# Gathering U and V rows apart: two rings in place of one in a mixture-of-single-neurons layer

## The reference

```python
q = (xt @ w_query).reshape(t, PEER_HEADS, 2, PEER_HALF)          # 8 heads
sk = jnp.einsum('thcd,ckd->thck', q, sub_keys)                    # 2 x 128 keys
top_s, top_i = lax.top_k(sk, PEER_TOPK)                           # 16 of each
cand_s, cand_i = all 16 x 16 sums and their expert numbers
best_s, best_pos = lax.top_k(cand_s, PEER_TOPK)                   # 16 experts per token and head
gate = jax.nn.softmax(best_s, axis=-1)
h = jnp.einsum('thkd,td->thk', peer_u[ib], xb)                    # a dot with a gathered U row
a = gb * jax.nn.gelu(h)
out = jnp.einsum('thk,thkd->td', a, peer_v[ib])                   # a sum of gathered V rows
```

## Time and profile before

| | us |
|---|---|
| median of 3 runs (2952.5 to 2953.97) | 2953.06 |
| the profiled execution | 2958.09 |
| its span | 2956.3 |
| PE busy, 71% of the span | 2096.2 |
| DVE busy, 70% | 2067.5 |
| POOL busy, 40% | 1191.8 |
| ACT busy, 35% | 1040.9 |
| the gather queue's packets, 87.7% of 16 engines' span | 1073.81 MB |
| the weight queue's packets, 8.3% | 97.07 MB |

### The profile page before, as it was taken

The page is one execution under the profiler, slowest core; times in us unless marked ns, Lnnn a source line. Parts: engine busy times, 40 slices in busy tenths (PEclk is TensorE's granted clock), DMA queues, the critical chain, the costliest instruction groups (busy, mean ns, idle before and its releaser), DMA issues.

```text
span 2956.3 us, 37239 instructions
## 1 busy us (share of the span) xinstructions
PE 2096.2 (71%) x12696; PEld 1037.4 (35%) x12696; DVE 2067.5 (70%) x5215; ACT 1040.9 (35%) x3347; POOL 1191.8 (40%) x1028
## 2 busy tenths in 40 slices
PE   8877788777776876586775877667777565566556
PEld 7544454343443442243332533234343111111111
DVE  3456678977567787867567678976766766777665
ACT  3322345633233445423233345632223222222222
POOL 0033334343344334443434434443444445444443
PEclk9899889798888887888987988888898768766876
DMA  6089999999999999999999999999999999999998
GB/s 239 29 324 419 419 420 419 389 420 420 419 417 420 420 415 413 417 383 420 420 420 421 414 382 420 421 385 420 420 419 421 421 421 420 421 415 420 416 417 337
DMA packets 174494, 1173.26 MB, mean 397 GB/s; under 512 B 19296, under 2 KB 19552, under 8 KB 43232
## 3 DMA queue, kind: packets, MB, share of 16 engines
q0 software_dynamic: 147456, 1073.81, 87.7%
q1 hardware_dynamic: 26848, 97.07, 8.3%
HBM read 1168.71 MB, written 2.10 MB: 396 GB/s over the span
## 4 chain that ended last, share of the span: by engine, by line
DMA 47%; PE 23%; DVE 18%; ACT 5%; issue 5%; POOL 2%; SPq 0%; DVEq 0%; ACTq 0%; POOLq 0%
DMA gather<-experts,idx 47%; PE ysum L691 12%; DVE gather L1268 9%; PE bank L469 6%; POOL gather L424 2%; ACT amp L924 2%; ACT diag L932 1%; PE ysum L477 1%; PE bank L666 1%; ACT gel L917 1%; DVE x L1244 1%; PE bank L518 1%; DVE scratch L1219 0%; DVE scratch L1215 0%; DVE ij L1220 0%
## 5 line engine op out<-in xcount | busy, mean ns | idle before, releaser
L424 POOL DMA_INDIRECT gather<-experts,idx x1024 | 1191.5, 1164 | 1742.4 <-PE ysum L691 1417.8
L691 PE MATMUL ysum<-gather,diag 64*64 64x512 f32 x8192 | 1256.1, 766 | 742.5 <-ACT diag L932 709.3
L1268 DVE CUSTOM_DVE_ANT_0 gather<-gather,xc 128x1024 f32<-128x1024 f32 x1024 | 1230.2, 1225 | 683.6 <-DMA gather<-experts,idx 680.6
L691 PEld LDWEIGHTS ysum<-gather,diag 64*64 64x64 f32 x8192 | 364.2, 171 | 1535.4 <-ACT diag L932 920.6
L917 ACT ACTIVATE gel<-hdot 128x4 f32<-128x4 f32 x255 | 52.4, 205 | 1684.2 <-DVE hdot L1268 1684.2
L469 PE MATMUL bank<-xnT,w 128*128 128x256 f32 (+1 forms) x2048 | 466.4, 384 | 4.9 <-DVE xnT L984 4.9
L469 PEld LDWEIGHTS bank<-xnT,w 128*128 128x128 f32 x2048 | 379.6, 194 | 99.2 <-issue 42.5
L932 ACT ACTIVATE diag<-cc,amp 128x64 f32<-128x64 f32 x1020 | 268.1, 333 | 0.4 <-PE ysum L691 0.4
L924 ACT ACTIVATE amp<-gel,gate 128x1 f32<-128x1 f32 x1020 | 216.9, 283 | 8.3
L917 ACT ACT_TABLE_LOAD x105 | 134.7, 1283 | 1.8
L666 PEld LDWEIGHTS bank<-w,yT 128*128 128x128 f32 x768 | 87.3, 192 | 17.1 <-issue 17.1
(11 more groups left out here) (127 smaller groups left out, 1502.6 us busy)
## 6 DMA issues: line engine op xcount, KB each, us to landing
w<-weights SPq DMA_DIRECT2D x164, 512.0 KB, 7.9
gather<-experts,idx POOLq DMA_INDIRECT x1024, 14.9
gather<-weights SPq DMA_DIRECT2D x4, 1024.0 KB, 5.6
y_out<-x SPq DMA_DIRECT2D x4, 512.0 KB, 7.9
x<-x_in SPq DMA_DIRECT2D x2, 512.0 KB, 4.5
g2b<-g_rows SPq DMA_DIRECT2D x2, 512.0 KB, 11.5
x<-x_in SPq DMA_DIRECT2D x1, 1024.0 KB, 12.4
cc<-consts_in SPq DMA_DIRECT2D x1, 856.0 KB, 9.7
```

What stands on the lines that cost most here:

```text
L424: pool.indirect_dma_start(gather[:, n % SLOTS, :], None, uv_d[m // 2], bass.IndirectOffsetOnAxis(ap=idx[:, g % 2, k:k + 1], axis=0)).then_ ...
L691: mm = nc.tensor.matmul(ysum[outs, q * 512:(q + 1) * 512], diag[toks, n % NDIAG, :], gather[toks, n % SLOTS, DM + hf * 512:DM + (hf + 1) * ...
L1268: e = V.tensor_tensor_reduce(out=gather[:, n % SLOTS, 0:DM], in0=gather[:, n % SLOTS, 0:DM], in1=xc[:, :], scale=1.0, scalar=0.0, op0=ALU. ...
```

## The change

The host no longer concatenates: U and V are tables of their own, with rows of 4 KB. The ring becomes two, `urows` with 8 slots and `vrows` with 12, of 4 KB per partition each; together they take as much memory as before. POOL issues the U gather of slot i and then the V gather of slot i - 4 (`ULEAD = 4`). A U slot is freed when the dots of its chunk are done (`s_h`, once per chunk), a V slot by its sum (`s_yc`). PE waits for the V landing itself (`s_gv`), and `route_experts` waits until the sums of the head two back are done before it overwrites `idx`, because V gathers read the indices later than U gathers. `wout` moves to V slots 4 to 11, `x2n` to U slot 7.

```diff
-SLOTS = 10
+USLOTS, VSLOTS = 8, 12
+ULEAD = 4
...
-        gather = sb("gather", SLOTS, 2 * DM)
+        urows = sb("urows", USLOTS, DM)
+        vrows = sb("vrows", VSLOTS, DM)
...
-            for m in range(NBLK):
-                for head in range(TT * HEADS):
-                    g = m * TT * HEADS + head
-
-                    pool.wait_ge(s_idx, g + 1)
-                    for k in range(TOPK):
-                        n = g * TOPK + k
-                        if n >= SLOTS:
-
-                            pool.wait_ge(s_yc, n - SLOTS + 1)
-                        elif n == WO:
-
-                            pool.wait_ge(s_oy, 4)
-                        pool.indirect_dma_start(
-                            gather[:, n % SLOTS, :], None, uv_d[m // 2],
-                            bass.IndirectOffsetOnAxis(ap=idx[:, g % 2, k:k + 1], axis=0)
-                        ).then_inc(s_g[n % SLOTS], 16)
+            slots = NBLK * CHUNKS * CH
+            for i in range(slots + ULEAD):
+                if i < slots:
+                    g, k = divmod(i, TOPK)
+                    if k == 0:
+                        pool.wait_ge(s_idx, g + 1)
+                    if i >= USLOTS:
+
+                        pool.wait_ge(s_h, (i - USLOTS) // CH + 1)
+                    pool.indirect_dma_start(
+                        urows[:, i % USLOTS, :], None, u_d[i // (2 * CHUNKS * CH)],
+                        bass.IndirectOffsetOnAxis(ap=idx[:, g % 2, k:k + 1], axis=0)
+                    ).then_inc(s_gu[i % USLOTS], 16)
+                n = i - ULEAD
+                if n >= 0:
+                    g, k = divmod(n, TOPK)
+                    if n >= VSLOTS:
+
+                        pool.wait_ge(s_yc, n - VSLOTS + 1)
+                    elif n == WO:
+
+                        pool.wait_ge(s_oy, 4)
+                    pool.indirect_dma_start(
+                        vrows[:, n % VSLOTS, :], None, v_d[n // (2 * CHUNKS * CH)],
+                        bass.IndirectOffsetOnAxis(ap=idx[:, g % 2, k:k + 1], axis=0)
+                    ).then_inc(s_gv[n % VSLOTS], 16)
...
+                pe.wait_ge(s_gv[n % VSLOTS], 16 * (n // VSLOTS + 1))
                 pe.wait_ge(s_dg, n + 1)
...
-                                              gather[toks, n % SLOTS, DM + hf * 512:DM + (hf + 1) * 512],
+                                              vrows[toks, n % VSLOTS, hf * 512:(hf + 1) * 512],
...
+            if g >= 2:
+
+                dve.wait_ge(s_yc, (g - 1) * TOPK)
             V.scalar_tensor_tensor(idx[:, g % 2, :], ij[:, 0, :], float(NKEYS), ij[:, 1, :], ALU.mult, ALU.add)\
                 .then_inc(s_idx, 1)
...
-                    dve.wait_ge(s_g[n % SLOTS], 16 * (n // SLOTS + 1))
-                    e = V.tensor_tensor_reduce(out=gather[:, n % SLOTS, 0:DM], in0=gather[:, n % SLOTS, 0:DM],
+                    dve.wait_ge(s_gu[n % USLOTS], 16 * (n // USLOTS + 1))
+                    e = V.tensor_tensor_reduce(out=urows[:, n % USLOTS, :], in0=urows[:, n % USLOTS, :],
...
-        arrays[f"experts{l}"] = np.concatenate([i["peer_u"][l], i["peer_v"][l]], axis=1)
+        arrays[f"u{l}"] = np.ascontiguousarray(i["peer_u"][l])
+    for l in range(DEPTH):
+        arrays[f"v{l}"] = np.ascontiguousarray(i["peer_v"][l])
```

More of the change, by code:

```diff
@@ L176, in item, with build @@
     return swa, t, h, (max(t - 1, 0) if swa else 0)
-def build(nc, x_d, wall_d, small_d, consts_d, g2b_d, late_d, uv_d, out_d):
+def build(nc, x_d, wall_d, small_d, consts_d, g2b_d, late_d, u_d, v_d, out_d):
     f32, u32 = mybir.dt.float32, mybir.dt.uint32
@@ L279, in build @@
         s_pw = sem("s_pw")
-        s_g = [sem(f"s_g{i}") for i in range(SLOTS)]
+        s_gu = [sem(f"s_gu{i}") for i in range(USLOTS)]
+        s_gv = [sem(f"s_gv{i}") for i in range(VSLOTS)]
         s_idx = sem("s_idx")
@@ L330, in head_start @@
             return mixer
-        WO = SLOTS - 4
-        wout = gather[:, WO:SLOTS, :].rearrange("p s (i c k) -> p (s i) c k", i=2, c=KD)
-        x2n = gather[:, WO - 1, 0:DM]
+        WO = VSLOTS - KD
+        wout = vrows[:, WO:VSLOTS, :].rearrange("p i (c k) -> p i c k", c=KD)
+        x2n = urows[:, USLOTS - 1, :]
         def interleave(m, mixer, peer, first, slices_first=False):
@@ L390, in _ @@
                     i = b - 8
-                    sp.dma_start(gather[:, WO + i // 2, :].rearrange("p (b c k) -> p b c k", b=2, c=KD),
+                    sp.dma_start(wout[:, i:i + 2, :, :],
                                  wall_d[0, NZ + NV + i:NZ + NV + i + 2].rearrange("b p c k -> p b c k")).then_inc(s_wout, 16)
@@ L1419 @@
     out = nc.dram_tensor("y_out", (SEQ, DM), mybir.dt.float32, kind="ExternalOutput").ap()
-    build(nc, *aps[:6], aps[6:], out)
+    build(nc, *aps[:6], aps[6:6 + DEPTH], aps[6 + DEPTH:], out)
     r = run(nc, [arrays], core_ids=[0])
```

## The result

The changed kernel took 3511.56 us, median of three (3495.83 to 3521.22), against 2953.06 us: a ratio of 1.188, 95% interval [1.186, 1.191]. The forecast was 3150 us, range 3030 to 3235. The direction was right, the size was not: 362 us are missing.

What follows compares the result with a forecast made beforehand. POOL was to become the bound at 2.89 us per slot: 164 before the first issue, 1024 x 2.89 = 2959, dips 20, end 11, span 3154 us; 3151 without a profile, rounded to 3150 us, range 3030 to 3235.

Steps and rivals of the forecast that it cites:

- the rings: U and V slots: U issues wait for earlier dots, V issues for sums; cost 0, or 0 to 3 us per head.
- the dips 20: Four dips of DMA from late DVE or PE pieces, which POOL cannot catch up: 20 us.
- if POOL waits long for the dots: Sign that the ring binds; the forecast kept the wait of U issues for dots under 100 us.
- the U ring binds: Rival, chance 0.11: late DVE stops POOL at the U ring, 3 us in each of 64 heads, 3340 us.
- POOL's issues: Two gathers issued per slot, each 0.94 us and 0.30 us to the next: 2.48 us per slot.
- The holds: Issues lengthened inside dots: per head 4.2 us in bursts and 2.4 us at single dots; 2.89 us per slot in all.
- DMA packets: Gathered rows of 4 KB cost 3.3% more: 0.08 us per slot, 82 us if DMA alone counts, bounds 0 and 120.
- DMA alone: Rival, chance 0.25: POOL falls into step and DMA alone sets the pace, 3035 us.
- Who holds whom: POOL against DVE: an issue that begins inside a dot is held to the dot's end; 0.94 us becomes 1.98 in bursts.
- the late V: PE's new wait on V, issued four slots after U: 0, up to 1 us per chunk.
- Faster: Rival, chance 0.08: earlier freed U rows and twelve V rows fill the four dips, DMA stays full, 2929 us.

Runs made afterwards that it cites:

- e10: The kernel before with a tiny second indirect gather (16 rows of 4 bytes) per slot, on a chip of the second kind: 3282.28 us, ratio 1.111.
- e6: The kernel before with a tiny second indirect gather (16 rows of 4 bytes) per slot, on the first kind of chip: 3002.47 us, ratio 1.016.
- e7: The changed kernel with 12 U slots and 8 V slots in place of 8 and 12, on the second kind of chip: 3260.39 us, ratio 1.103.
- e20: The changed kernel with only half of each V row gathered and used twice, on the first kind of chip: 3170.30 us, ratio 1.073.
- e1: The changed kernel unaltered, timed again on the first kind of chip: 3112.26 us, ratio 1.053.
- e18: The changed kernel with the dot replaced by a sum over the U row (one SBUF input), on the first kind of chip: 3023.81 us, one run.
- e3: The changed kernel with ULEAD = 0, V of a slot issued right after its U, on the first kind of chip: 3092.88 us, ratio 1.048.
- e17: The kernel before with a tiny second gather on even slots only, on the first kind of chip: 2964.87 us, ratio 1.005.
- e19: The kernel before with a tiny second gather on even slots only, again on the first kind of chip: 2966.46 us, ratio 1.004.
- e13: The kernel before with 960 tiny transfers from SP's queue, six after each weight load, on the second kind of chip: 2974.34 us, ratio 1.007.
- e5: The changed kernel with the dot replaced by a sum over the U row (one SBUF input), on the second kind of chip: 3579.16 us, ratio 1.212.
- e8: The changed kernel unaltered, timed again on the second kind of chip: 3460.64 us, ratio 1.169.
- e16: The changed kernel with the dot replaced by a sum over the U row (one SBUF input), on the second kind of chip: 3589.19 us.
- e15: The changed kernel unaltered, timed to tell the kind of chip, which was the second: 3448.06 us.

## Why the prediction was wrong, step by step

*What failed.* The step was the rings: "Cost taken: 0; if the cover is gone, 0 to 3 us per head", and the sum's "the dips 20". At the first timing POOL waited 458 us, 7 us per head, not 0 to 3: 352 ahead of U issues, and 106 ahead of V issues, which had been put at 0 as well. By the prediction's own sign ("if POOL waits long for the dots", over 100 us; it was 314) this is the ring. The cover that the step counted on, 5 to 10 us for DVE to be late, was gone because the engines themselves ran slow in stretches. The runs lay that at POOL's doubled gathers, on one of two kinds of chip (e10 against e6: 3282 against 3002 us for the same kernel). Nothing in the trace of before could show it. The rival "the U ring binds" had the mechanism by which it became time (e7: four more U slots give back 200 us) and was priced at 190 us over the forecast, 3340; it had no cause for DVE being that late.

*What held on the first kind of chip*, where the kernel takes 3112 us against the forecast of 3150. It is that close because two misses are of opposite sign, holds 121 us under and waits 70 over:

- POOL's issues: 0.94 + 0.30 us each, 2540 us forecast, 2547 found, on both kinds.
- The holds: 422 forecast, 440 where POOL alone sets the pace (e20, 3170 us), 301 where DMA is full as well (e1). With rows waiting in a queue the dots shift against the issues, and fewer are caught: 652 issues of over 0.98 us in e1, 768 in e20. That the queue is the reason is my reading. That it is the dots that hold the issues is shown by e18: one input, 13 us.
- DMA packets: 3.3% taken, and full stretches read 409 GB/s against 421, 2.9%. The figure of the Trainium skill, 408.7 GB/s for 4 KB rows ("DMA: Bandwidth & Descriptors", "iDMA fabric — 4 AXI ports for 8 engines, asymmetric across TPBs"), is met.
- "DMA alone", 3035 us: e18 gives 3024. It was the right price of a case that doesn't occur, since POOL's holds keep it from the floor.
- Who holds whom: in e1 475 issues start inside a dot with over 0.2 us of it left and are held, 25 that start in its first 0.05 us are not. The dots that start inside an issue are not held (750 of them, 1223 ns on average, 1253 at most). The rule of the Trainium skill on two SBUF inputs ("SBUF — State Buffer", "SBUF: two separate sides") has whichever starts second blocked for the whole instruction; e1 and e18 bear it out for the issues and not for the dots.
- The rings, the lead and the late V: waits of 90 us in all; split alone 3088, no lead 3093, changed 3112. The changed rings and lead, which were to help, cost 24 us there (the ratios' intervals, [1.051, 1.055] and [1.043, 1.049], don't overlap), 19 of them by the lead (e3).
- Faster: never near. Of the splitting's 135 us (3088 against 2953), 49 come with the doubled issues at 0.85 us for the second one (e6, 3002), and the rest with its 0.94 us.

One reading of the rows was off: the full slices of the kernel before stand at 413 to 421 GB/s, not 422; no term hangs on it.

*What stays open.* Why two kinds of chip differ; whether the number of POOL's gathers or their unbroken cadence brings the slow stretches (e17 and e19 never met the second kind; that one input is slower than the changed kernel there speaks for the cadence); and whether the recording has a part in them, since on that kind half of the semaphore updates are missing from the trace of every slow kernel, and a sixth of the landings from e13's, which is hardly slow. No run here was without a record of its clock and span.

## What to carry to other kernels

An engine that idles because it waits for slots can be the next bound: count its instructions after the change, with their gaps and with what holds them, before counting on its idle time. Splitting one indirect gather into two buys finer release at 1.24 us of POOL per gather, and more where DVE runs instructions with two SBUF inputs beside it. A change that doubles what a software queue is asked to do should be timed on more than one chip; here one chip said 5% and another 19%, and the kernel before did not tell them apart. And a ring's slack should be set against the latest consumer in a bad stretch and not against its mean.

## What the runs showed that was not expected

Chips of one type gave the same time for one kernel within 0.1% (2951 to 2953 us) and 3112 against 3448 to 3512 us for another. On the slower kind, chained instructions of DVE that take no wait before were 0.6 to 3.2 us apart, and matmuls without waits 1.4 to 2.8 us.

Taking 300 us of holds off POOL made the kernel 119 to 141 us slower on the slower kind of chip (e5 beside e8, e16 beside e15), and 88 us faster on the other (e18 against e1).

An indirect gather of 16 rows of 4 bytes occupies POOL for 0.85 us where nothing holds it, one of 128 rows of 4 or 8 KB for 0.94: the price is the instruction, hardly the rows.
